# Modulation tiles summed by VectorE after transposes, and decay exponents formed one slot earlier

## What is computed

```
m_lat = (silu(c)    @ w_ada + b_ada)            # 6 x 2048 values
m_ctx =  silu(c_ctx) @ w_ada + b_ada
sh1, sc1, g1, sh2, sc2, g2 = split(m_lat, 6)
u = rmsnorm(x) * (1 + sc1) + sh1

# delta rule of one head (q, k normalised to length 1)
cum_g = cumsum(g)
gamma = exp(where(lower, cum_g[i] - cum_g[j], -1e30))
a_mat = where(strict, (k*beta) @ k.T * gamma, 0)
u, w  = triangular solves with a_mat + I
qk    = q @ k.T * gamma
```

## Time and profile before

| | us |
|---|---|
| runs | 3319.96, 3325.28, 3327.51 (median 3325.28) |
| the profiled execution | 3323.27, its span 3321.4 |
| TensorE busy in the span | 3186.8 (96%) |
| VectorE, ScalarE, GpSimd busy | 1909.2 (57%), 1605.9 (48%), 1967.4 (59%) |
| mean granted clock | 0.981 |

### The profile page before, as it was taken

How to read it: one execution, slowest core, us unless ns; L and a number is a source line. 1 busy time by engine, 2 the same in 40 slices (tenths; PEclk the granted TensorE clock), 3 DMA queues, 4 the chain that set the end, 5 groups by cost and what they waited for, 6 DMA issues and landing times.

```text
span 3321.4 us, 59787 instructions
## 1 busy us (share of the span) xinstructions
PE 3186.8 (96%) x21428; PEld 2911.8 (88%) x21428; DVE 1909.2 (57%) x3133; ACT 1605.9 (48%) x2379; POOL 1967.4 (59%) x2680
## 2 busy tenths in 40 slices
PE   7999999999999999999998989999999999999998
PEld 6999999999988888888866989999987888888887
DVE  5566655656577755764766874555456543434344
ACT  5545544455445444444434655656553534444443
POOL 4766776777545555555533557878763555555553
PEclk8999999999999999999998999999999999999999
DMA  6666666666675555555635777677667455555553
GB/s 219 210 228 201 224 216 214 232 202 223 219 250 188 187 184 184 188 184 183 189 128 184 254 235 237 213 215 233 209 223 268 160 185 188 187 184 188 183 186 120
DMA packets 262848, 672.98 MB, mean 203 GB/s; under 512 B 28311, under 2 KB 66936, under 8 KB 262008
## 3 DMA queue, kind: packets, MB, share of 16 engines
q1 hardware_dynamic: 262584, 669.55, 61.1%
HBM read 663.12 MB, written 6.32 MB: 202 GB/s over the span
## 4 chain that ended last, share of the span: by engine, by line
PE 74%; DVE 9%; POOL 7%; issue 4%; DMA 3%; ACT 3%; SPq 1%; DVEq 0%; POOLq 0%; ACTq 0%
PE psum L707 28%; PE psum L708 14%; POOL w_lo L553 7%; PE psum L700 6%; PE psum L702 6%; PE psum L701 6%; PE psum L705 2%; PE psum L1662 1%; DVE psum L531 1%; DVE work L951 1%; PE psum L1670 1%; PE psum L704 1%; ACT w_hi L540 1%; DVE work L1539 1%; DMA raw<-w_ada 1%
## 5 line engine op out<-in xcount | busy, mean ns | idle before, releaser
L553 POOL TENSOR_TENSOR w_lo<-raw,w_hi 128x256 fp32r<-128x256 f32 x2676 | 1967.2, 768 | 1331.6 <-ACT w_hi L540 1330.3
L540 ACT ACTIVATE w_hi<-raw 128x1024 fp32r<-128x1024 f32 (+3 forms) x1112 | 1051.1, 948 | 1262.9 <-PE psum L702 509.7
L707 PE MATMUL psum<-act_a,w_hi 128*128 128x512 f32 x2535 | 911.8, 402 | 16.7 <-DVE act_a L937 10.6
L553 DVE TENSOR_TENSOR w_lo<-raw,w_hi 128x1024 fp32r<-128x1024 f32 (+2 forms) x332 | 413.9, 1247 | 545.8 <-ACT w_hi L540 545.3
L708 PE MATMUL psum<-act_a,w_lo 128*128 128x256 f32 x2535 | 715.2, 282 | 0.0
L707 PE MATMUL psum<-act_b,w_hi 128*128 128x512 f32 x1856 | 668.5, 402 | 7.3 <-DVE act_b L941 5.3
L700 PE MATMUL psum<-act_a,w_lo 128*128 128x256 f32 x2048 | 605.5, 296 | 12.5 <-DVE act_a L941 9.4
L707 PEld LDWEIGHTS psum<-act_a,w_hi 128*128 128x128 f32 x2535 | 479.4, 189 | 133.0 <-issue 14.0
L702 PE MATMUL psum<-act_a,w_hi 128*128 128x256 f32 x2048 | 583.1, 285 | 0.0
L701 PE MATMUL psum<-act_a,w_hi 128*128 128x256 f32 x2048 | 582.6, 284 | 0.0
L708 PE MATMUL psum<-act_b,w_lo 128*128 128x256 f32 x1856 | 523.6, 282 | 0.0
(11 more groups left out here) (373 smaller groups left out, 3574.7 us busy)
## 6 DMA issues: line engine op xcount, KB each, us to landing
raw<-w_mlp SPq DMA_DIRECT2D x256, 512.0 KB, 4.1
raw<-w_up SPq DMA_DIRECT2D x176, 512.0 KB, 3.6
raw<-w_dil SPq DMA_DIRECT2D x192, 384.0 KB, 3.4
work<-w_ada SPq DMA_DIRECT2D x288, 256.0 KB, 4.0
raw<-w_hg SPq DMA_DIRECT2D x128, 320.0 KB, 3.1
raw<-w_delta SPq DMA_DIRECT2D x64, 512.0 KB, 4.2
raw<-w_out SPq DMA_DIRECT2D x64, 512.0 KB, 5.3
raw<-w_down SPq DMA_DIRECT2D x64, 512.0 KB, 3.6
```

Of the source, the lines that this page charges most:

```text
L540: act.activation(w_hi[:, t % SPLIT, 0:nb * P], raw[:, t % RAW, 0:nb * P], ACT.Copy)\
L553: ins = eng.tensor_tensor(w_lo[:, t % SPLIT, cols], raw[:, t % RAW, cols], w_hi[:, t % SPLIT, cols], ALU.subtract)
L707: pe.matmul(bank, wh, src[:, kt, :], start=first, stop=False)
```

## The change

Two things.

First, the modulation tile's end: TensorE now transposes the four 128x128 chunks of `ada_row` into the whole bank (4 transposes with 128 columns in place of 4 matmuls with one), and VectorE sums each row of a chunk from PSUM (a reduction of 128x512 to 128x4), waits for its own result through the new semaphore `ada_sum`, and adds the bias.

Second, the exponents: VectorE forms them in slot 8, ahead of the Newton steps, and ACT takes their exponential in slot 9, straight behind the guess, in place of slot 12. ACT's wait for `delta_kq`, ahead of the row decays, is new.

```diff
@@ ada_finish, TensorE
-                    ins = eng.matmul(to[:, c:c + 1], ada_row[:, c * P:(c + 1) * P], ones[:, 0:1],
-                                     start=True, stop=True)
+                    ins = eng.transpose(to[:, c * P:(c + 1) * P], ada_row[:, c * P:(c + 1) * P], ident)
@@ ada_finish, VectorE
-                eng.tensor_tensor(mod[:, part, bass.ds(n * 4, 4)], ada_bank(ph)[:, 0:4],
+                eng.tensor_reduce(mod[:, part, bass.ds(n * 4, 4)], A2(ada_bank(ph), a=4), AX.X, ALU.add)\
+                   .then_inc(sem("ada_sum"), 1)
+                wait(eng, "ada_sum", turned + 1)
+                eng.tensor_tensor(mod[:, part, bass.ds(n * 4, 4)], mod[:, part, bass.ds(n * 4, 4)],
                                   gains[:, bass.ds(n * 4 + 96, 4)], ALU.add)\
                    .then_inc(sem("ada_mod"), 1)
@@ delta_act
                           "delta_guess")
-                yield
-                yield
-                yield
                 wait(act, "delta_diff", i + 1)
                 act.activation(d_e, d_e, ACT.Exp).then_inc(sem("delta_gamma"), 1)
+                yield
+                yield
+                yield
+                wait(act, "delta_kq", i + 1)
                 for d in range(2):
@@ delta_dve
                    .then_inc(sem("delta_silu"), 1)
                 yield
+                wait(dve, "bc_loaded", i * 16 + 16)
+                for d in range(2):
+                    for k in range(2):
+                        ins = dve.scalar_tensor_tensor(
+                            d_e[:, d, :, k * P:(k + 1) * P], d_bc[:, d, :, k * P:(k + 1) * P],
+                            d_gs[:, 2 * d + k:2 * d + k + 1],
+                            A2(neg[:, 2 * d * P:(2 * d + 2) * P], a=2), ALU.add, ALU.add)
+                ins.then_inc(sem("delta_diff"), 1)
                 yield
                 wait(dve, "delta_guess", i + 1)
...
                                          ALU.mult, ALU.mult).then_inc(sem("delta_kq"), 1)
-                wait(dve, "bc_loaded", i * 16 + 16)
-                for d in range(2):
-                    for k in range(2):
-                        ins = dve.scalar_tensor_tensor(
-                            d_e[:, d, :, k * P:(k + 1) * P], d_bc[:, d, :, k * P:(k + 1) * P],
-                            d_gs[:, 2 * d + k:2 * d + k + 1],
-                            A2(neg[:, 2 * d * P:(2 * d + 2) * P], a=2), ALU.add, ALU.add)
-                ins.then_inc(sem("delta_diff"), 1)
```

More of the change, by code:

```diff
@@ L1439, in gen @@
                           "delta_guess")
+                wait(act, "delta_diff", i + 1)
+                act.activation(d_e, d_e, ACT.Exp).then_inc(sem("delta_gamma"), 1)
                 yield
@@ L1442, in gen @@
                 yield
-                wait(act, "delta_diff", i + 1)
-                act.activation(d_e, d_e, ACT.Exp).then_inc(sem("delta_gamma"), 1)
+                wait(act, "delta_kq", i + 1)
                 for d in range(2):
```

## The result

The changed kernel took 3303.61 us (median of 5 runs, 3302.14 to 3308.15), the kernel before 3325.28 in the same five rounds (3318.41 to 3327.51): 21.7 us less, ratio 0.994, with a 95% interval from 0.993 to 0.9951. The forecast was 3304. The profiled execution of after is the longest of its five, 3308.15 us (span 3306.4), so against the earlier trace rows its trace shows only 15.0 us. Where those are, and why single terms of the forecast were some 5 us off while their sum came out, is the subject here.

A forecast was written before the change was run, and what follows sets the result against it. TensorE, busy 96% of the span, was taken as the bound. Exponents -11.6 and -2.0, transposes -10.0, reduction +2.5 sum to -21.1 us, from a median of 3325.3 to about 3304; range 3294 to 3317.

The forecast's parts named there:

- The gap of slot 9: VectorE's waits for `w_ada` and the guess in phase "one" would be filled by the exponent pieces: 11.6 us over 8 heads.
- So all of it is won at line 1648.: Each filled gap is smaller than TensorE's wait for `delta_z0` in its head, so the wait shrinks by it: -11.6 us.
- the edit costs nothing there: ACT's later split in slot 9 delays GpSimd, but 1.8 us of slack remain before TensorE needs its item: 0 us.
- The second effect: Some exponent pieces in slot 8 would lie free of GpSimd and run shorter: -2.0 us, bounds nothing and 9.5 us.
- New waits at line 1639: Later `delta_kq` makes TensorE wait under 1 us in two or three heads, not added, since the `delta_z0` wait shrinks equally.
- Transposes: At the modulation tile ends, four transposes take 0.44 us on TensorE, not 0.81: 0.37 at 27 of 32 tiles, -10.0 us.
- The reduction: VectorE's sum from PSUM at tile ends takes 0.69 us and lies on the path at five tiles: together +2.5 us.
- The sum.: Whole kernel: -11.6 - 2.0 - 10.0 + 2.5 = -21.1 us, giving a median of about 3304.
- rivals 1, 2 and 4: `w_ada` gap reopens: 3318, chance 0.13; transposes don't overlap: 3322, 0.06; ACT's stall starves GpSimd, then TensorE: 3327 and more, 0.04.
- rival 3: The reduction delays TensorE at many more tiles ("ctx", slot 18 of "one") or costs 1.2 us: +10 us, 3314; chance 0.12.

The follow-up runs named there:

- The run in slot 9: The changed kernel with the four exponent pieces behind slot 9's two modulation pieces, still ahead of the guess: 3305.64 us, ratio 0.9949 to the kernel before.
- the second trace: The changed kernel itself, unaltered, run again beside the kernel before on another chip: 3300.68 us, ratio 0.9944.
- The delay of `delta_z0`: The changed kernel with the last product ahead of `delta_z0` (line 1567) made four times in place of once: 3329.01 us, ratio 1.0023 to the kernel before.

## Why the prediction was right in its time, and where its steps were wrong

- **The gap of slot 9.** Right as a mechanism: the gaps from slot 9 to `delta_z0`, 11.6 us in 8 heads, are all gone, as forecast. VectorE's waits for `w_ada` between 60 and 880 us went from 23.1 to 12.4 us, and nearly all that is left is slot 8's. The run in slot 9 confirms it: there they are 24.0.
- **"So all of it is won at line 1648."** Wrong. The step that failed is the one on ACT: "the edit costs nothing there". I asked whether TensorE would wait for `w_lo`, and it does not. I didn't ask what GpSimd's later run would lie beside. It lies beside line 1562, +5.6 us in 8 heads. 11.6 and the pieces' 1.8 less 5.6 are the 7.8 measured. In the second trace the same sum is 5.2 (0.1 and 6.5) and 6.9 were measured, so it closes to 2 us. I had also left ACT's table load of 1.28 us out of slot 9; in the second head it ran while the pieces were being made, and the split came 2.1 us late where I had 2.6.
- **The second effect**, free pieces, was sized at 2.0 and gave 1.8 us in one trace (26.0 to 24.2) and 0.1 in the other (25.9), inside its bounds. The mechanism itself was far stronger than I made it, in a place to which I hadn't applied it, and with the other sign.
- **A term was missing**: three falls of the clock behind waits of 2.61 us and more, 4.4 us. It nearly cancels the 5.6. The delay of `delta_z0` proves the kind of effect, with 1.3 to 1.4 us a fall.
- **New waits at line 1639**: under 1 us each as forecast, in fact 0.01 to 0.24 us more in heads 2 to 7, 0.9 us together; in the second trace in the second head alone, 0.09.
- **Transposes**: 0.45 a tile in place of 0.37. "Two", where two kernels with the old ends took 526.6 and 528.4, takes 523.0 to 523.5 in eight traces with the new ones and 525.0 to 526.3 in four: 3 to 5 us in most, 3.0 forecast. In "one" 14 tiles gave 2.3 us without the exponents' move and 8 with it (726.0 to 717.7). Their own worth is 6.3 us both times; the difference is the clock, which ran at the lower level for 10 us more in the first case and 3.4 less in the second. The forecast took the parts as independent.
- **The reduction**: 0.68 as forecast (0.69). Its cost was put at 2.5 us net in five places; "ctx" alone costs 2 to 3 us against before, since one of its scans is pushed beside GpSimd too. At the end of "one" the new tile end costs nothing (1.69 us from its start to the next product, before and after), in "out2" 0.3 (2.28 and 2.58). The last stage is 1.3 longer in all (754.8 to 753.5), but so it is without the reduction (754.9) and with products with ones in "out2" (755.0): the other 1 us is not the reduction's.
- **The sum.** By the stages of the second trace of after: heads -14.8, to "out" -2.8, "ctx" +2.4, "two" -5.1, the end +1.3, the start -0.5: 19.5 us without the stage that the change doesn't touch. The forecast's 21.1 was met by luck of the sum: an overrated term (7.8 in place of 13.6 at line 1648) and an underrated price in "ctx" were made up by the clock, which the forecast didn't have, and by cheaper transposes. The rivals 1, 2 and 4 did not occur; rival 3 in a small form, in "ctx" alone.

What stays open: why the clock fell behind two of three waits of 2.14 us in one kernel and one of 1.80 in another, and behind none of 2.40 and 2.43 in the kernel before; and whether the 9 us between the medians of the changed kernel and the one with the exponential in slot 12, taken on different chips, are more than the 3.3 that the heads show.

## What to carry to other kernels

When a change makes one engine wait in a new place, follow the work that it feeds: the question is not only who starves, but beside which instructions of a third engine the delayed work now runs. Here ACT's 2.3 us in slot 9 moved GpSimd's run over a VectorE line with two SBUF inputs and took back 5.6 of the 11.6 us won; leaving the exponential in slot 12 gives them back, at the price of 1.7 us of waits. And weigh a wait of TensorE by what its clock does behind it: here the waits of 2.6 to 3.8 us for `delta_z0` cost 1.3 to 1.5 us each beyond their length, while those up to 1.7 cost only themselves. Two changes that look independent can be coupled through it.

## What the runs showed of the hardware that was not expected

- A two-input product from SBUF (128x256) takes 430 ns beside an idle GpSimd and up to 976 beside one that is busy throughout; the exponent piece 0.48 and 0.95; a product with one input in PSUM takes 415 either way.
- A stall of ACT can make a kernel faster for VectorE: with GpSimd starved for 4.8 us, four pieces took 1.67 us in place of 3.11.
- With the clock's falls counted, TensorE's busy time over 700 us of seven heads agrees to 1 us among the traces of the same tile ends (two with the old, four with the new); each stretch of 3.4 us at 1.2 GHz adds 1.3 to 1.5 us.
- Two traces of one program agree within 0.2 us over the 718 us of seven heads, where TensorE rarely stops, while 14 traces spread over 10 us in the 870 of MLP and filter, which were the same in all and where the clock moves. A profiled execution says where time goes, but its own total may be 9 us off the median (3307.18 against 3298.32).
